# A fused attention and expert layer: adaLN rows on two engines, staggered first blocks, key sums added up ahead of TensorE, and an earlier last row

## The reference

```
h = adaLN(RMSNorm(x)); proj = h @ w_in     # window q|k|v, stick-breaking q|k|v, gates
A: sliding-window attention with rotary and sinks
B: stick-breaking attention, per block of 128 queries:
   z = q k^T / 8;  log_1mb = where(causal, log_sigmoid(-z), 0)
   after = reverse_cumsum(log_1mb) - log_1mb           # sum over LATER keys
   a = exp(where(causal, log_sigmoid(z) + after, -inf));  o = a v
x += gate1 * ((sigmoid(ga) * A @ w_up_swa + sigmoid(gb) * B @ w_up_sb) @ w_out)
x += gate2 * peer(adaLN(RMSNorm(x)))       # 8 heads, 16 of 16384 experts each
return RMSNorm(x)
```

## Time and profile before

| what | value |
|---|---|
| median of 3 runs | 1735.62 us |
| profiled execution | 1736.6 us, its span 1734.8 us |
| TensorE busy | 1688.3 us (97%) |
| VectorE busy | 1373.4 us (79%) |
| ScalarE, GpSimd busy | 715.0 us (41%), 640.4 us (37%) |
| mean granted TensorE clock | 0.992 |

### The profile page before, as it was taken

How to read it: one execution, slowest core, us unless ns; L and a number is a source line. 1 busy time by engine, 2 the same in 40 slices (tenths; PEclk the granted TensorE clock), 3 DMA queues, 4 the chain that set the end, 5 groups by cost and what they waited for, 6 DMA issues and landing times.

```text
span 1734.8 us, 24253 instructions
## 1 busy us (share of the span) xinstructions
PE 1688.3 (97%) x8795; PEld 1492.4 (86%) x8795; DVE 1373.4 (79%) x2770; ACT 715.0 (41%) x1117; POOL 640.4 (37%) x372
## 2 busy tenths in 40 slices
PE   6899999999999999999999999999999999999997
PEld 4677877878799999899999999999999988888886
DVE  7446655674489999999999488888878799988887
ACT  2356536543444343444444343333333343333333
POOL 1222312325337564611111055555534454334330
PEclk9899999999999999999999999999999999999999
DMA  7322242334043432567777799999988899999992
GB/s 314 111 108 86 98 166 102 133 122 146 3 155 118 146 129 96 160 209 285 287 284 270 285 378 351 338 360 330 341 319 303 274 387 407 397 384 387 376 389 106
DMA packets 162156, 417.97 MB, mean 241 GB/s; under 512 B 13584, under 2 KB 83216, under 8 KB 156176
## 3 DMA queue, kind: packets, MB, share of 16 engines
q1 hardware_dynamic: 113680, 266.88, 42.4%
q0 software_dynamic: 36864, 134.23, 21.1%
q10 hardware_dynamic: 11520, 15.73, 2.5%
HBM read 373.80 MB, written 42.99 MB: 240 GB/s over the span
## 4 chain that ended last, share of the span: by engine, by line
PE 82%; DVE 14%; ACT 1%; issue 1%; DMA 1%; POOL 1%; SPq 0%; DVEq 0%; ACTq 0%
PE bank L937 29%; PE bank L889 23%; PE bank L678 10%; PE bank L836 5%; PE bank L925 5%; DVE arena L1571 1%; PE bank L625 1%; PE bank L704 1%; PE bank L767 1%; DVE slots L1503 1%; PE bank L746 1%; DVE slots L1499 1%; DVE idx L1510 1%; DVE arena L1329 1%; PE bank L759 1%
## 5 line engine op out<-in xcount | busy, mean ns | idle before, releaser
L889 PE MATMUL bank<-h_split,u_split 128*128 128x384 f32 x3072 | 557.2, 337 | 3.8 <-POOL u_split L572 2.6
L889 PEld LDWEIGHTS bank<-h_split,u_split 128*128 128x128 f32 x3072 | 534.8, 188 | 10.3 <-POOL u_split L572 4.3
L937 PE MATMUL bank<-v_late,a_late 128*128 128x512 f32 x1440 | 326.7, 389 | 0.0
L937 PEld LDWEIGHTS bank<-v_late,a_late 128*128 128x128 f32 x1440 | 270.3, 188 | 56.0
L590 POOL DMA_INDIRECT rows<-eu,idx x128 | 180.0, 1407 | 361.0 <-DVE dots L1492 338.5
L590 POOL DMA_INDIRECT rows<-ev,idx x128 | 174.3, 1361 | 243.5 <-DVE row_sum L1598 212.1
L562 POOL TENSOR_TENSOR block_split<-arena,block_split 128x1024 fp32r<-128x1024 f32 x50 | 122.2, 2448 | 313.1 <-ACT block_split L1002 313.1
L1151 ACT ACTIVATE gelus<-bank 128x384 f32<-128x384 f32 x128 | 63.0, 492 | 373.7 <-PE bank L889 373.6
L937 PE MATMUL bank<-v_split,a_split 128*128 128x512 f32 x864 | 205.4, 391 | 0.0
L937 PEld LDWEIGHTS bank<-v_split,a_split 128*128 128x128 f32 x864 | 161.5, 188 | 32.0
L1598 DVE SCALAR_TENSOR_TENSOR row_sum<-rows,agate,row_sum 128x1024 f32<-128x1024 f32 x127 | 162.6, 1280 | 4.1
(11 more groups left out here) (244 smaller groups left out, 2360.6 us busy)
## 6 DMA issues: line engine op xcount, KB each, us to landing
u_raw<-euT SPq DMA_DIRECT2D x128, 512.0 KB, 6.6
v_raw<-ev SPq DMA_DIRECT2D x128, 512.0 KB, 6.7
arena<-w_blocks SPq DMA_DIRECT2D x50, 512.0 KB, 9.3
arena<-w_ada SPq DMA_DIRECT2D x12, 2048.0 KB, 8.2
gates_scratch<-stage SPq DMA_DIRECT2D x24, 1024.0 KB, 10.2
gates<-gates_scratch SPq DMA_DIRECT2D x64, 384.0 KB, 8.1
gelu_scratch<-gelus ACTq DMA_DIRECT2D x80, 192.0 KB, 3.5
gelus<-gelu_scratch SPq DMA_DIRECT2D x80, 192.0 KB, 8.2
```

Of the source, the lines that this page charges most:

```text
L889: last = pe.matmul(ps[6 + b][:, 0:TD], us[:, b, wp, k * P:(k + 1) * P], hs[:, xp, k, 0:TD], start=(k == 0 and q == 0), stop=(k == DC - 1 a ...
L937: last = pe.matmul(ps[2 * t + f][:], a[:, ap, t * P:(t + 1) * P], v[:, vp, f * 512:(f + 1) * 512], start=(first and q == 0), stop=True, sk ...
```

## The change

1. Of adaLN group 3 VectorE multiplies six key parts, TensorE the last two (`ADA_DVE = 6`), into bank 5; the row is copied and turned like that of group 2 and added in the bank. VectorE makes products 0 and 1 ahead of `inv_rms(1)`; `spread(1)` stands behind the direct products; two chunks instead of four are normed ahead of the bias.
2. In the first two blocks, block 1 runs three chunks behind block 0.
3. The sum over later keys for key block 0: VectorE adds up the softplus of key blocks 1, 2 and 3 (`later`), splits it, and TensorE multiplies it once by ones (384 columns, high and low) instead of blocks 1, 2 and 3 one by one.
4. `later_sums` stands ahead of `turn_probs` on TensorE, and the attention's exponentials ahead of the probT copies on ScalarE (`later` lies in probT's place).
5. `row_total(0, 3)` moves to value chunk NK - 4 and `row_sums(0, 3)` to NK - 2.

```diff
-            spread(1)
             pe.wait_ge(cact_ready, 1)
-            pe.wait_ge(ring_in[0], 16)
-            for k in range(DC):
-                last = pe.matmul(ps[4][0:1, :], cact[:, k:k + 1], ring[:, 0, ...], ...)
-            last.then_inc(ada_direct, 1)
+            for slot, bank, first in ((0, 4, 0), (3, 5, ADA_DVE)):
+                pe.wait_ge(ring_in[slot], 16)
+                for k in range(first, DC):
+                    last = pe.matmul(ps[bank][0:1, :], cact[:, k:k + 1], ring[:, slot, ...], ...)
+                last.then_inc(ada_direct, 1)
+            spread(1)
             ada_sum(1, 1, ps[6], 4)
...
-            for k in range(DC):
-                pe.wait_ge(h1_split, k + 1)
-                for t in range(2):
+            for k, t in [(j - 3 * t, t) for j in range(DC + 3) for t in range(2)]:
+                if 0 <= k < DC:
...
+                    terms = {0: [(0, from_r, 0), (P, all_r, 3)], 1: [(0, from_r, 1), (P, all_r, 2)], 2: [(0, from_r, 2)], 3: []}[b]
+                    for first, keys, c in terms:
+                        for half in (sp_hi + [later_hi], sp_lo + [later_lo]):
+                            last = pe.matmul(at[:, first:], keys, half[c], start=False, stop=b == 0, ...)
...
-                        turn_probs(n)
                         later_sums(n)
+                        turn_probs(n)
...
+                sa.wait_ge(sp_ready, 5 * n + 5)
+                act_(later_hi, later, ACT.Copy).then_inc(sp_hi_ready, 1)
...
+                ve.wait_ge(sp_ready, 5 * n + 4)
+                nv.tensor_copy(later[:, 0:P], spl[1][:, 0:P])
+                step(nv.tensor_tensor(later[:, P:], spl[1][:, P:], spl[2], ALU.add))
+                nv.tensor_tensor(later[:, 2 * P:], later[:, 2 * P:], spl[3], ALU.add).then_inc(sp_ready, 1)
+                for k in range(4):
+                    ve.wait_ge(sp_hi_ready, 4 * n + k + 1)
+                    nv.tensor_tensor((sp_lo + [later_lo])[k], (spl[0:3] + [later])[k], (sp_hi + [later_hi])[k].bitcast(F32), ALU.subtract).then_inc(sp_split, 1)
...
+                if i == NK - 4:
+                    row_total(0, 3)
```

More of the change, by code:

```diff
@@ L739, in later_sums @@
                     at = ps[bank][:, col:col + T - b * P]
[L740 to L746, removed]
+                    terms = {0: [(0, from_r, 0), (P, all_r, 3)], 1: [(0, from_r, 1), (P, all_r, 2)], 2: [(0, from_r, 2)], 3: []}[b]
+                    for first, keys, c in terms:
+                        for half in (sp_hi + [later_hi], sp_lo + [later_lo]):
+                            last = pe.matmul(at[:, first:], keys, half[c], start=False, stop=b == 0, skip_group_check=True)
+                    if b:
+                        of_key = K_NTRI if b == 3 else K_NONE
+                        last = pe.matmul(at[:, (3 - b) * P:], cst[:, of_key:of_key + P], spl[3], start=False, stop=True, skip_group_check=True)
                     last.then_inc(sb_summed, 1)
@@ L802, in _ @@
                             rotate(i + 1)
+                        later_sums(n)
                         turn_probs(n)
-                        later_sums(n)
                     block(AT[b], BANK[AT[b]])
@@ L1036, in _ @@
             act_(cosT, cosT, ACT.Sin).then_inc(trig_ready, 1)
-            sa.wait_ge(ada_direct, 1)
-            act_(arow[0:1, :], ps[4][0:1, :], ACT.Copy).then_inc(ada_row, 1)
+            for b in range(2):
+                sa.wait_ge(ada_direct, b + 1)
+                act_(arow[0:1, b, :], ps[4 + b][0:1, :], ACT.Copy).then_inc(ada_row, 1)
             block_high(0)
@@ L1084, in _ @@
                 block_high(t0 + 3)
+                for k, b in enumerate(SB_ORDER):
+                    bank, col = SB_AT[b]
+                    sa.wait_ge(sb_summed, 4 * n + SB_WHOLE[k])
+                    act_(atB[b], ps[bank][:, col:col + T - b * P], ACT.Exp).then_inc(at_ready, 1)
                 sa.wait_ge(probT_done, n + 1)
@@ L1278, in _ @@
                     v_high(i + 2)
+                if i == NK - 2:
+                    row_sums(0, 3)
                 if i == NF:
@@ L1282, in _ @@
                         act_(g2b[:, f * 512:(f + 1) * 512], ps[6 + f][:], ACT.Copy).then_inc(g2_ready, 1)
[L1284 to L1292, removed]
+            row_sums(1, 0)
+            row_sums(2, 1)
             for f in range(2):
@@ L1327, in ada_product @@
                 step(nv.tensor_scalar(adap[:, b, :], w[:, 0, :], cact[:, 0:1], None, ALU.mult))
-                for k in range(1, DC):
+                for k in range(1, parts):
                     ins = nv.scalar_tensor_tensor(adap[:, b, :], w[:, k, :], cact[:, k:k + 1], adap[:, b, :], ALU.mult, ALU.add)
-                    if k < DC - 1:
+                    if k < parts - 1:
                         step(ins)
@@ L1373, in _ @@
             for k in range(DC):
-                if k + 4 < DC:
-                    normed(k + 4)
+                if k + 2 < DC:
+                    normed(k + 2)
                 ve.wait_ge(h_ready, k + 1)
@@ L1663, in _ @@
                 v_low(i + 1)
[L1664 to L1672, removed]
             def row_total(n, t):
@@ L1686, in row_total @@
                 nv.tensor_tensor(xT2[t], xT2[t], z[t], ALU.add).then_inc(z_ready, 1)
+            weights(NF)
+            a_low(NF)
+            for i in range(NF, NK):
+                if i + 1 < NK:
+                    weights(i + 1)
+                    v_low(i + 1)
+                    a_low(i + 1)
+                for k in range(accs_before(i), accs_before(i + 1)):
+                    add_row(k)
+                if i == NK - 4:
+                    row_total(0, 3)
             def row_scale(n, t):
```

59 lines of the change are left out of this document (34 added, 25 removed).

## The result

| kernel | median | range, executions |
|---|---|---|
| before | 1735.81 us | 1734.94 to 1736.73, 19 |
| changed | 1739.09 us | 1736.41 to 1739.73, 19 |

The ratio is 1.0015, 95% interval 1.0008 to 1.0022: by the bound of 0.2% that the prediction set, no change, with a small loss that the interval keeps apart from zero. The forecast was 1737.7 with a range of 1731.0 to 1742.5. The profiled execution took 1739.73, its span 1737.9, so against the profiled one of before (1736.6, span 1734.8) the sum to explain is +3.1.

What follows compares the result with a forecast made beforehand. TensorE, 97% busy, bounds the kernel where it never pauses; VectorE sets the pace at the start, in heads 0, 1, 3, 5 and at the end. -4.4 + 7.6 - 1.1 = +2.1: 1737.7 us median, range 1731.0 to 1742.5.

Steps and rivals of the forecast that it cites:

- start: adaLN's start and first two blocks: block 0 starts at 48.1 and ends earlier; -4.4 us, gain bounds 3.5 to 5.4.
- heads, waits less TensorE's saving: Eight heads: VectorE's added work lengthens waits in heads 0 to 6, head 7 saves 0.4; +7.6 us, bounds 4.5 and 12.9.
- heads, granted clock: Heads: no clock loss was forecast for TensorE's pauses; 0 us.
- end: Last value chunks: expert row's total moves earlier, VectorE takes tile 1 sooner; -1.1 us, bounds 0 and 1.1.
- The heads, VectorE: Four new operations ahead of evacuation and rotation: 1.5 us more per odd head, 1.4 per even; bounds 1.0 and 2.2.
- The heads, TensorE: Fewer products save 0.37 us per head, 3.0 over eight; in seven heads this only lengthens TensorE's wait.
- The rival of cover: Heads: VectorE's extra work finds cover, TensorE's saving counts in full; -8.5 us, 1727.1; chance 0.12.
- The lost race: Even heads: GpSimd starts before the last low part and holds it, TensorE waits 2.1 each; +8.5, 1746.2; chance 0.10.
- The low clock: First two blocks: gaps keep TensorE at 0.50, start gives at most 1 us; +3.5, 1741.2; chance 0.13.

Runs made afterwards that it cites:

- measured alone: Kernel before with only parts 1 and 2 (start), 1730.64 us; only parts 3 and 4 (heads), 1745.12 us; only part 5 (end), 1734.82 us.
- the runs with VectorE off the path: Changed kernel, second evacuation and rotation ahead of VectorE's adaLN product, SyncE's weight loads ahead of the adaLN load: 1724.14 us; the same without part 3: 1727.85 us.
- the run that loses it: Changed kernel with one more VectorE addition of 384 columns between the third and the last low part of each head: 1760.60 us.
- the heads alone: Kernel before with parts 3 and 4 of the change only: 1745.12 us, ratio 1.0052.
- transposes first again: Changed kernel with the transposes of the probabilities ahead of the sums again on TensorE, ScalarE's order left as changed: 1738.95 us.
- high parts between the row copies: Changed kernel with ScalarE making the first two weight blocks' high parts between the two row copies: 1739.00 us.

## Why the prediction was right, and where it was not

The time lay within the range, 1.4 above the forecast, and most of the mechanism came as described. The sum, step by step, for the profiled execution:

| term | forecast | profile | measured alone |
|---|---|---|---|
| start | -4.4 | -3.9 | -5.2 |
| heads, waits less TensorE's saving | +7.6 | +6.5 | |
| heads, granted clock | 0 | +1.7 | |
| heads together | +7.6 | +8.2 | +9.2 |
| end | -1.1 | -1.1 | -1.0 |
| sum | +2.1 | +3.1 | +3.0 |

The 8.2 of the heads is read from positions: at block 2 the change is 3.9 ahead, at TensorE's first wait behind the heads (358.32 before, 364.27 now) 5.95 behind. Two low stretches are 3.4 of these 9.9, which leaves 6.5.

- **The start: right in mechanism.** The new queue on TensorE set its end, `mul1` was held until GpSimd's pair ended, and block 0 started at 48.55 where 48.1 was forecast. The direct products took 11.51 instead of 10.8: they began 2 us earlier, but the half passes kept 0.85 each until 33.5 (before, until 32.9) and 0.43 only from then on, so the early start cost 1.6 and not 0.8. GpSimd's pair ended at 46.22; 40.9 + 5.08 in the prediction gives 46.0, not its 45.7. Block 0 was over at 60.3 instead of 59.7, because it began 0.45 later and the clock rose at 54.5, 5.9 us after its start (53.5 was forecast). Gain 3.9. Alone it measured 5.2: in that profile TensorE's first block started 1.05 earlier than in the change, 0.76 of it because `mul1` was not held. How the three engines meet there differs from one profile to the next, more than the prediction's one order of events allowed for: the direct products end between 38.3 and 39.9 in the eleven profiles of kernels with the new start.
- **The heads, VectorE: right in odd heads, too much in even ones.** In odd heads 1.5 more, added to the waits, gave 2.6 forecast and 2.6 measured; positions of `later_sums` from head 5 to head 6, where no clock stretch falls, moved by 1.45. In even heads 1.4 was forecast and 1.15 came: the four operations put the adaLN product 1.4 later, but its first operation then stands 0.23 less for GpSimd (head 2, before and in the change, rows below). TensorE's positions moved by 1.12 in head 0 and by 0.58 in heads 2, 4 and 6, where 1.4 and 0.7 were forecast; that is 0.6 of the 1.1 between 7.6 and 6.5.

```profile
173.37 2.24 DVE L1327 TENSOR_SCALAR arena<-arena,cact 128x512 f32<-128x512 f32 x1
174.89 2.01 DVE L1344 TENSOR_SCALAR arena<-arena,cact 128x512 f32<-128x512 f32 x1
```

- **The heads, TensorE: right, and of little weight.** The prediction took 0.37 per head for the products that go; the runs with VectorE off the path show 3.7 / 8 = 0.46. In the seven heads with a wait the saving only lengthens the wait, as the prediction had it, so the difference counts in head 7 alone.
- **The heads, granted clock: the step that failed.** The prediction counted a wait at its length. Two of the three long pauses cost 1.7 more each, and one stretch of before (at 360.5) fell away: net +1.7 in this profile. It also fits the groups into which the 19 executions fall: 1736.4 and 1736.6 at a mean clock of 0.994, six from 1737.3 to 1738.0 at 0.992 or 0.993, eleven from 1739.0 to 1739.7 at 0.991 or 0.992. Without its +1.7 the profiled execution would stand at 1738.0, beside the middle group.
- **The rival of cover** is out: TensorE resumed where the rotation ended, and part 3 cost 9.7. **The lost race** did not happen, by 0.26 where 0.3 was reckoned. It was priced at 8.5 for a margin lost by a little; the run that loses it shows 21.5, of which 8.2 are waits. The price counted neither the clock nor that the waits ahead of the fourth block would go. Its condition was put wrongly in one point: additions ahead of ScalarE's copy move GpSimd too. **The low clock** at the start did not come: at 0.50 until 54.5, then 1.00. The chunks did come 1.66 apart, but the gaps that this rival reckoned with hardly show: TensorE was busy 5.73 of the 5.80 us up to 54.3. **The end** came as worked out.

That start and heads both came out larger than forecast when measured alone (-5.2 and +9.2) and cancel is luck: the total was nearer than its parts.

The Trainium skill, "SBUF — State Buffer", section "Who interferes with whom", calls the contention of VectorE and GpSimd an exclusive lock, in which the order of issue and not the shape of the operation decides who blocks. The trace agrees: 8 columns were held for 0.76 us and 384 columns for 2.05, each time behind a GpSimd operation that had begun first.

## What to carry to other kernels

Work added on an engine that is 79% busy can cost more than it saves on one that is 97% busy: what counts is what it stands ahead of on its own engine, and who waits there. Before giving such a change up, move the waited-for operations ahead of the work nobody waits for, and then look at what that work releases at its end; here a slot, on whose release a queue of unrelated loads stood. The same part 3 was worth -3.7 us with VectorE's and SyncE's order mended and +9.7 in the order of the change.

## What the runs showed of the hardware

- **A short pause of TensorE can cost its clock.** In every profile read here, each low stretch between the first blocks and the end began 1.6 to 5.3 us behind the start of a pause of 0.7 to 3.5 us in otherwise dense work; it was 3.4 us long (twice or three times that in four of some fifty cases) at 0.50, a loss of 1.7 us. Not every pause has one: in the profile of the change heads 1 and 3 lost it (2.6 us of pause each), head 5 with the same pause did not, and pauses of 0.7 mostly did not. Of the twelve waits of 2.6 us for the rotation in four profiles (the change, the heads alone, transposes first again, high parts between the row copies) seven lost it, as did eight of the fourteen pauses of 2.6 us near 700 us, one in each profile. So they cost about 1 us more than their length on the average, and the time of such a kernel can fall into steps. That the pause brings the clock down is read from this order in all profiles; a pause by itself was not tried.
- **VectorE's hold behind GpSimd came for small and large operations alike**: `mul1`, 128 by 8, stood until GpSimd's pair had ended (0.93 us instead of 0.17), a low part of 384 columns for 2.60 instead of 0.55.
